# Projection weights of two head groups in chunks of 1024 columns, each loaded in two parts

## The reference

```
z = einsum('btd,df->btf', u, w_qkv).reshape(b, t, 3 groups, q/k/v, 16 heads, 64)
q = rms_norm(z[..., 0], q_gain);  k = rms_norm(z[..., 1], k_gain);  v = z[..., 2]
```

## Time and profile before

| what | value |
|---|---|
| runs | 1174.26 us median (1172.14 to 1175.84) |
| profiled execution | 1171.47 us, of which the span of its instructions 1169.7 us |
| PE busy | 1081.0 us (92%) |
| DVE, POOL, ACT busy | 432.5, 239.8, 216.1 us |
| DMA | 462.66 MB in packets, mean 396 GB/s |
| DMA queue of SP (q1) | 440.29 MB, 94.8% of 16 engines' span |
| DMA queue of POOL (q0) | 18.75 MB, 4.2% |
| granted TensorE clock | 0.953 |

### The profile page before, as it was taken

The page is one execution under the profiler, slowest core; times in us unless marked ns, Lnnn a source line. Parts: engine busy times, 40 slices in busy tenths (PEclk is TensorE's granted clock), DMA queues, the critical chain, the costliest instruction groups (busy, mean ns, idle before and its releaser), DMA issues.

```text
span 1169.7 us, 14221 instructions
## 1 busy us (share of the span) xinstructions
PE 1081.0 (92%) x4991; PEld 654.3 (56%) x4991; DVE 432.5 (37%) x843; ACT 216.1 (18%) x532; POOL 239.8 (21%) x504
## 2 busy tenths in 40 slices
PE   7899999999954999998999999999689899999995
PEld 4688888888831788873444344445443344443443
DVE  4356755755740476242221121112850112221212
ACT  2222122122210244131111111112121011111110
POOL 1013222321320122005211222220322222112220
PEclk9999999999967699998999999999799899999998
DMA  9999999999999999999999999999999999999998
GB/s 359 354 372 396 379 389 385 403 394 401 388 364 369 359 341 348 370 404 382 425 430 428 429 433 426 423 440 423 378 388 356 429 427 432 426 428 427 431 416 270
DMA packets 63754, 462.66 MB, mean 396 GB/s; under 512 B 11452, under 2 KB 19404, under 8 KB 47092
## 3 DMA queue, kind: packets, MB, share of 16 engines
q1 hardware_dynamic: 50992, 440.29, 94.8%
q0 software_dynamic: 5424, 18.75, 4.2%
q10 hardware_dynamic: 7284, 2.87, 1.0%
HBM read 454.99 MB, written 183.21 MB: 546 GB/s over the span
## 4 chain that ended last, share of the span: by engine, by line
PE 58%; DMA 6%; DVE 5%; issue 2%; ACT 1%; ACTq 0%; DVEq 0%; SPq 0%
PE bank L1322 28%; PE bank L1288 9%; PE bank L1346 5%; DMA ring_lo<-in_cache_kv_w_dram 3%; DMA ring_lo<-in_w_up_dram 3%; PE bank L1234 2%; PE bank L1297 2%; PE bank L1193 2%; PE bank L1201 1%; PE bank L1213 1%; PE bank L1304 1%; PE bank L1190 1%; PE bank L309 1%; PE bank L1166 1%; PE bank L1335 1%
## 5 line engine op out<-in xcount | busy, mean ns | idle before, releaser
L1322 PE MATMUL bank<-ring_lo,scratch 128*64 128x512 f32 x1024 | 344.5, 605 | 3.9 <-DMA ring_lo<-in_w_up_dram 3.9
L1120 PE MATMUL bank<-uT,ring_lo 128*128 128x264 f32 x1152 | 269.9, 388 | 0.5 <-DVE uT L323 0.5
L1120 PEld LDWEIGHTS bank<-uT,ring_lo 128*128 128x128 f32 x1152 | 214.6, 191 | 39.0 <-issue 1.2
L1322 PE MATMUL bank<-region_a,scratch 128*64 128x512 f32 x512 | 231.4, 606 | 0.0
L1322 PEld LDWEIGHTS bank<-ring_lo,scratch 128*64 128x64 f32 x1024 | 106.1, 139 | 147.5 <-issue 147.2
L833 DVE RECIPROCAL scratch<-scratch 128x264 f32<-128x264 f32 x48 | 86.5, 1803 | 97.5 <-ACT scratch L675 97.4
L1288 PE MATMUL bank<-scratch 128*128 128x512 f32 (+1 forms) x216 | 110.9, 640 | 3.1 <-DVE scratch L988 3.1
L1322 PEld LDWEIGHTS bank<-region_a,scratch 128*64 128x64 f32 x512 | 68.6, 139 | 65.9 <-issue 64.0
L1013 DVE TENSOR_TENSOR scratch<-bank,scratch 128x512 f32<-128x512 f32 x16 | 11.1, 692 | 243.5 <-PE bank L1322 243.5
L1020 DVE TENSOR_TENSOR hT<-bank,hT 128x264 f32<-128x264 f32 x128 | 55.4, 433 | 120.0 <-PE bank L1346 118.6
L583 POOL TENSOR_TENSOR small<-epsc 128x1 f32<-128x1 f32 x71 | 13.7, 195 | 363.5 <-PE bank L1304 347.9
(11 more groups left out here) (228 smaller groups left out, 1121.0 us busy)
## 6 DMA issues: line engine op xcount, KB each, us to landing
out_dram<-in_cache_kv_w_dram SPq DMA_DIRECT2D x124, 1023.5 KB, 19.8
ring_lo<-in_w_up_dram SPq DMA_DIRECT2D x28, 2048.0 KB, 21.3
ring_lo<-in_w_qkv_dram SPq DMA_DIRECT2D x18, 2048.0 KB, 21.8
out_dram<-in_cache_kv_w_dram SPq DMA_DIRECT2D x32, 1022.0 KB, 20.9
ring_lo<-in_w_gate_dram SPq DMA_DIRECT2D x14, 2048.0 KB, 12.9
region_a<-in_w_gate_dram SPq DMA_DIRECT2D x14, 2048.0 KB, 17.4
region_a<-in_w_down_dram SPq DMA_DIRECT2D x14, 2048.0 KB, 13.1
ring_lo<-in_w_down_dram SPq DMA_DIRECT2D x14, 2048.0 KB, 17.6
```

Of the source, the lines that this page charges most:

```text
L1120: last = mm(z_bank[i % 4][:, 0:T], w[:, k, at:at + P], uT[:, k, :], start=(k == 0), stop=(k == KT - 1))
L1322: last = mm(out[rows, :], lhs[:, k, rows], weights[e][w][:, k, columns], start=(k == 0), stop=(k == k_tiles - 1))
```

## The change

The weights of groups 0 and 1 (tiles 0 to 47) come in 6 chunks of 1024 columns, eight tiles each. A chunk is two loads of 2 MB by feature rows: part 0 holds feature tiles 0 to 3, part 1 holds 4 to 7, each partition with 4 runs of 4 KB. Even chunks go to slots 0 and 1, odd ones to slot 2 and to `extra`, a slot's size in the room where group 2's queries and keys will be kept. Every tile of these groups reads both parts, so TensorE waits for part 0 ahead of the tile's first matmul and for part 1 ahead of its fifth. Group 2 keeps its six chunks of 512 columns. The copies are put anew between the loads: 14 are begun ahead of chunk 2, then 3 behind each part, then 3 behind each chunk of group 2: 56 by the end of the loop, so 11 are left for the end.

```diff
+    WIDE = (G - 1) * NZ // (2 * TPC)
+        extra = region_a[:, (G - 1) * 2 * KT * T:(G - 1) * 2 * KT * T + SLOT]
+        extra_full = sem("extra_full")
-        COPIES = {"first_chunks": 7, "chunk": (3, 3, 3), ...
+        COPIES = {"first_chunks": 9, "wide": (3, 3), "chunk": (3, 3, 3), ...
-        RING_KV = CHUNKS // 3
+        RING_KV = WIDE // 2 + 2
+        def wide_slot(c, part):
+            if part:
+                return (slot(1), ring_full[1]) if c % 2 == 0 else (extra, extra_full)
+            return (slot(0), ring_full[0]) if c % 2 == 0 else (slot(2), ring_full[2])
+        def of_tile(tile, k):
+            if tile < WIDE * 2 * TPC:
+                c = tile // (2 * TPC)
+                w, full = wide_slot(c, k // 4)
+                at = tile % (2 * TPC) * P
+                return w.rearrange("p (k n) -> p k n", k=4)[:, k % 4, at:at + P], full, 16 * (c // 2 + 1)
+            c = tile // TPC
+            at = tile % TPC * P
+            return slot(c % 3).rearrange("p (k n) -> p k n", k=KT)[:, k, at:at + P], ring_full[c % 3], 16 * (WIDE // 2 + (c - 2 * WIDE) // 3 + 1)
+        wide_chunks = w_qkv[0].rearrange("(s k p) (c n) -> c s p k n", s=2, p=P, n=2 * CW)
-            for c in range(3):
-                sp.dma_start(slot(c).rearrange("p (k n) -> p k n", k=KT), qkv_chunks[c]).then_inc(ring_full[c], 16)
+            def wide_load(c, part):
+                w, full = wide_slot(c, part)
+                sp.dma_start(w.rearrange("p (k n) -> p k n", k=4), wide_chunks[c, part]).then_inc(full, 16)
+            for part in range(2):
+                wide_load(0, part)
             sp.wait_ge(bias_parts_landed, 32)
-            move_next(5)
+            move_next(1)
+            wide_load(1, 0)
+            move_next(2)
+            wide_load(1, 1)
+            move_next(2)
             sp.wait_ge(bias_stored, 16)
             move_next(COPIES["first_chunks"])
-            for c in range(3, CHUNKS):
-                sp.wait_ge(z_ready, (c - 2) * TPC)
+            for c in range(2, WIDE):
+                sp.wait_ge(z_ready, (c - 1) * 2 * TPC)
+                for part in range(2):
+                    wide_load(c, part)
+                    move_next(COPIES["wide"][part])
+            for c in range(2 * WIDE, CHUNKS):
+                sp.wait_ge(z_ready, (WIDE - 1) * 2 * TPC if c < 2 * WIDE + 2 else (c - 2) * TPC)
                 sp.dma_start(slot(c % 3).rearrange("p (k n) -> p k n", k=KT), qkv_chunks[c]).then_inc(ring_full[c % 3], 16)
                 move_next(COPIES["chunk"][c % 3])
-                    c = s // TPC
-                    if s % TPC == 0:
-                        pe.wait_ge(ring_full[c % 3], g * 32 + 16 * (c // 3 + 1))
                     for k in range(KT):
+                        w, full, count = of_tile(i, k)
+                        if k % 4 == 0 and i % TPC == 0:
+                            pe.wait_ge(full, count)
-                        last = mm(z_bank[i % 4][:, 0:T], w[:, k, at:at + P], uT[:, k, :], start=(k == 0), stop=(k == KT - 1))
+                        last = mm(z_bank[i % 4][:, 0:T], w, uT[:, k, :], start=(k == 0), stop=(k == KT - 1))
```

More of the change, by code:

```diff
@@ L276, in tiles_until @@
             return (count - 1) // NQK * NZ + (count - 1) % NQK + 1
-        COPIES = {"first_chunks": 7, "chunk": (3, 3, 3), "last_chunks": 3, "sample_half": (2, 0), "head": (1, 2), "heads_end": 4,
+        COPIES = {"first_chunks": 9, "wide": (3, 3), "chunk": (3, 3, 3), "last_chunks": 3, "sample_half": (2, 0), "head": (1, 2), "heads_end": 4,
                   "pair_0_early": (2, 1), "pair_0_late": ((2, 2), (2, 1)), "pair": ((1, 0, 0), (1, 0, 1)),
@@ L1109, in _ @@
                     g, s = divmod(i, NZ)
-                    c = s // TPC
-                    if s % TPC == 0:
-                        pe.wait_ge(ring_full[c % 3], g * 32 + 16 * (c // 3 + 1))
                     if i >= 4:
                         pe.wait_ge(zn_ready, i - 3)
-                    w = slot(c % 3).rearrange("p (k n) -> p k n", k=KT)
-                    at = s % TPC * P
                     for k in range(KT):
+                        w, full, count = of_tile(i, k)
+                        if k % 4 == 0 and i % TPC == 0:
+                            pe.wait_ge(full, count)
                         if i == 0:
                             pe.wait_ge(u_ready, k + 1)
-                        last = mm(z_bank[i % 4][:, 0:T], w[:, k, at:at + P], uT[:, k, :], start=(k == 0), stop=(k == KT - 1))
+                        last = mm(z_bank[i % 4][:, 0:T], w, uT[:, k, :], start=(k == 0), stop=(k == KT - 1))
                     last.then_inc(z_ready, 1)
```

## The result

The changed kernel takes 1179.65 us (median of 7 runs, 1172.35 to 1182.12); the kernel before, on the same chip, 1173.67 us (7 runs, 1169.45 to 1177.1). The ratio is 1.0049, 95% interval 1.0028 to 1.0071: slower by some 6 us, where 1.5 us of gain were forecast and the range ended at 1178.9. Later medians come from several chips, on which the kernel before takes 1167 to 1175 us, so only ratios to the kernel before on the same chip are compared.

The account below looks back on a forecast made before the run. SP's always-busy DMA queue was taken to set the end. Packets -3.0, low queue +1.2 and put-off copy +0.3 gave -1.5 us, so 1174.26 became 1172.8 us for the median, range 1168.0 to 1178.9.

Parts of the forecast that it names:

- the second parts: Projections, chunks 2 to 5: part 1 lands just in time; TensorE 0.5 us late in all, bounds -1 to 6.
- cost TensorE, not the queue: Projections: TensorE's waits for second parts add nothing to the sum as long as SP's queue has work.
- What bounds the kernel: Whole kernel: SP's queue always has work and sets the end; compute engines are done 9 us before the copies.
- Longer packets: Weight loads of groups 0 and 1: 4 KB instead of 2 KB packets save 3.0 us, between 0 and 5.0.
- Rival B: Weight loads: packets save nothing, 2 KB and 4 KB runs move alike; sum +0.3, 1174.6 us; chance 0.15.
- The start: Tile 0 now needs 4 MB; its fifth matmul is 0.7 us late, hidden behind ACT's first square: no cost.
- Where the queue runs low: Near 242.4 and 332.9 us: SP's queue is nearly dry when the next load is released; +1.2 us together.
- The put-off copy: End of kernel: the eleventh copy costs 3.3 us there against 3.0 in the projections: +0.3 us.
- Rival D: Projections: second parts 2 us later, TensorE 6 us late at tile 52, queue dry: +4.6, 1178.9 us; chance 0.18.
- the sum of what it moves: SP's queue: loads and copies land one after another, so the end is their sum plus any empty time.

Follow-up runs that it names:

- after: The first profiled execution of the changed kernel, the fastest of its seven runs: 1172.35 us.
- again: The changed kernel run once more, unchanged, for a second trace: ratio 1.0059 to the kernel before, 1181.21 us; its profiled execution took 1183.67 us.
- copy_back: The changed kernel with ten instead of nine copies in the first run of copies, 57 in the projections: ratio 1.0065, 1181.89 us.
- runs_2k: The changed kernel with each part fetched by two 1 MB loads in runs of 2 KB: ratio 1.0042, 1179.66 us.
- before_again: The kernel before, run once more unchanged for a second trace: ratio 1.0009.
- before_56: The kernel before with six instead of seven copies behind the store of the bias, one put off to the end: ratio 1.0011.
- before_58: The kernel before with one more copy behind chunk 14, moved from the end into the projections: ratio 0.9979, 1165.45 us beside 1167.06.
- late_due: The changed kernel with part 0 used twice in the first four tiles of chunks 2 to 5, so part 1 is due later; output differs: ratio 1.0050.
- by_columns: The changed kernel with each wide chunk's two loads being old chunks of 512 columns in 2 KB runs, the second due four tiles later: ratio 1.0023.
- early_58: early_parts with one more copy behind chunk 14, 58 in the projections: ratio 1.0018 to the kernel before.
- clear_58: clear_57 with one more copy behind chunk 14, 58 in the projections: ratio 1.0003 to the kernel before.
- parts_together: The changed kernel with the three copies between the two parts of chunks 2 to 5 moved behind the second part: ratio 1.0115, 1187.12 us.
- by_columns_57: by_columns with ten instead of nine copies behind the store of the bias, 57 in the projections: ratio 0.9996 to the kernel before.
- early_parts: The changed kernel with seven instead of nine first copies and one more behind part 1 of chunks 3 to 5, pulling second parts forward: ratio 1.0037.
- clear_57: The changed kernel with 57 copies placed anew, eight first and one instead of three behind part 1 of chunk 3: ratio 1.0010.
- keys_2k: The kernel before with POOL's cached keys loaded in runs of 2 KB instead of 4 KB, two loads for one: ratio 1.0022.

## Why the prediction was wrong

The step that failed is the second parts. Their waits are in the sum with nothing, as "0.5 us late in all" that "cost TensorE, not the queue"; in the runs TensorE lost 1.8 us (after), 7.0 (`again`) and 10.6 (copy_back) between tiles 8 and 64, and the queue lost with it. The gain of 3.0 us that was set against this didn't come.

- **What bounds the kernel**: right. The last copy ended last in every trace read for it.
- **Longer packets, -3.0**: mis-sized. The 6144 packets went, but in the packets of the traces' first 200 us one of 4 KB of SP's queue takes 177 ns after, two of 2 KB take 181 before: 6144 x 4 ns / 16 = 1.5 us. The 165 ns were read where the output weights come, with other traffic beside them. q1's total fell by 1108.9 - 1108.6 = 0.3 us, with a rounding of about 0.6 on each, and runs_2k is no slower than `again`. Rival B, that the packets save nothing, fits this within the noise; so does the rule of the Trainium skill, page "DMA: Bandwidth & Descriptors", section Specifications (line rate from 512 B on), that the prediction put aside.
- **The start**: right; tile 0 waited 0.46 us for part 1. That the store of the bias could come earlier and "the second parts hold TensorE back" was written, and not priced.
- **The second parts**: this step failed. The landings were right to 0.1 us at chunk 2 and 1.6 us at chunk 4 (161.3 against 162.9), but "I take 0.5 us late in all" compared them with one execution's TensorE. Tile 16 begins at 95.8 in before and before_again, at 91.2 and 92.0 in before_56 and before_58, whose start is the same. TensorE reaches its fifth matmul between 90.64 + 1.95 = 92.6 us (copy_back) and 96.9 (after), the part lands at 97 to 101 in after, `again` and copy_back, and a wait of 4.5 us costs another 2 through the clock. 4.54 + 2 us in `again` lie beyond the bounds of -1 to 6, 8.42 in copy_back more so.
- **"These waits cost TensorE, not the queue, as long as the queue has work"**: wrong in effect. In `again` tile 64 began at 296.3, and the first half of the output weights landed at 369.2 + 12.5 = 381.7. In before_56, which also starts early and has as many copies ahead, the two are 288.6 and 376.5: the queue lost 5.2 us.
- **POOL's key loads**: missing. The prediction counted what lies ahead of each weight load, not what other queues pass beside it. The weight load of chunk 7, now part 1 of chunk 3, came 3.5 us earlier (133.4 to 129.9), and the last keys then pass beside copies. In the two traces of the changed kernel this cost DVE and not TensorE; it cost TensorE 1.58 us in late_due and more where the parts come earlier still.
- **Where the queue runs low, +1.2 for two places**: it does at 242 us, by 0.25 to 1.35 us.
- **The put-off copy, +0.3**: too small, as far as the runs tell. One copy less in the projections cost 0.27% in by_columns (1.0023 against 0.9996) and 0.11% in before_56; one more gave 0.21% in before_58, 0.19% in early_58 and 0.07% in clear_58: 0.8 to 3.2 us. Only before_58 is clear of noise by itself; the signs agree. copy_back is no test of it, since its copy stands ahead of a part that is late already.
- **Rival D** had the sign and nearly the time, 1178.9, for its late parts. The time is in part luck: its empty queue is 1.35 us of it at most, and it does not know of the keys.

How TensorE's lateness reaches a queue that is hardly ever empty shows in the DMA view from 0 to 297 us, about the end of the projections (queue, packets, MB, share); before, then `again`:

```profile
...
q1 hardware_dynamic: 20851, 98.46, 87.2%
...
```

```profile
...
q1 hardware_dynamic: 14626, 96.96, 86.6%
...
```

The queue had moved 1.50 MB less, some 4.7 us at 3.3 us for a copy of 1.05 MB. Only 297 x 0.006 = 1.8 us of it is a lower share; in the rest the engines were busy and moved less. In the first trace after it is 97.51 MB, in parts_together 95.84, in by_columns_57 98.83. So "the sum of what it moves" has no fixed price. Why the same bytes took longer was not tested and stays open.

by_columns, which holds the order, the put-off copy and the low queue, costs 0.23%, or 2.7 us. What the changed kernel costs beyond it, 1.0049 to 1.0059 less 1.0023, is 0.26 to 0.36%, or 3.1 to 4.2 us, and is put down to TensorE held by parts or keys. This is what is left between two ratios and no sum of terms measured one by one, and the smaller of the two is hardly clear of noise. Parts and keys pull against each other: with parts earlier (early_parts) the keys are late, with parts later (copy_back) the parts are. By columns the second load is due four tiles later, and one place suits both. How the 3 to 4 us divide between parts and keys changes with the execution and was not settled.

## What to carry to other kernels

Pulling a load forward also moves what stands behind it: ask which transfers of other queues pass beside it, and whether they then meet packets of 64 KB instead of 2 KB. Splitting weights along the contraction makes the second half due at once; splitting along the columns makes it due half a chunk later, and here that slack was worth more than longer runs (0.9996 in by_columns_57 against 1.0065 in copy_back). And a margin read from one execution is no margin: look for what moves the consumer from run to run.

## What the runs showed of the hardware

The same key loads of 0.5 MB took 7.4 to 9.4 us from issue to landing with little beside them (clear_57), 9.8 to 11.0 beside weights in runs of 2 KB (before) and 20.8 to 25.0 beside a row of copies (parts_together). In the two windows of 4 us above the queues moved as many packets as each other, whatever the size; that a queue's price beside copies goes by its packets and not by its bytes was not tested, for keys_2k doubled the key packets beside weights only. And the kernel before itself moves by several microseconds from run to run: 1169.87 to 1179.25 us in 26 runs on the chip of before_again. Windows of its profile, then of its second profile:

```profile
...
620.00:640.00 20.00, 19.90 (x84) 7.26 (x79) 2.77 (x4) 1.79 (x3) 0.58 (x3) 1.00 1.00 428
...
```

```profile
...
620.00:640.00 20.00, 17.77 (x62) 7.13 (x64) 2.76 (x4) 1.78 (x3) 0.57 (x3) 0.91 1.00 423
...
```

In the second TensorE loses 19.90 - 17.77 = 2.1 us there. Expert weights that landed at 569 us come 4.9 us later in it. In again, runs_2k, late_due and by_columns too these loads fall behind on the way to 569 us, and hardly in the first profile of after; what causes it stayed open, and nothing here was run to find out. It is why a profile of 1171 us and one of 1184 us can't be set against each other without the medians.
